# Two blocks on one core: recurrent levels one tile later, rotations between projected tiles, tails among attention blocks, bias rows as eight-row pieces

## The reference, cut to what matters

```
# first block, per direction
dt = softplus(dt_raw + dt_bias);  a_cum = cumsum(dt * A)          # per head and chunk
lmat = exp(segsum(a)) ; y_diag = (C B^T * lmat) @ (x * dt)
# second block, per layer (x2)
z = rmsnorm(h) @ w_in                                             # 18 tiles of 128 features
o_a = rmsnorm(hgrn2(hq, hf, hi, lb)) * sigmoid(hg)                # recurrent, 4 heads of 64
o_b = attention(rope(aq), rope(ak), av, sinks)                    # window 128, 8 heads, 2 kv heads
o_c = gelu(su) * (W_s @ layernorm(gelu(sv)) + b_s)                # spatial gating
h = h + rmsnorm(concat(o_a, o_b, o_c) @ w_out)
```

## Time and profile before

| | |
|---|---|
| median of 3 runs | 2760.44 us (2758.29 to 2760.99) |
| profiled execution | 2757.06 us |
| its span, first to last instruction | 2755.2 us |
| mean granted TensorE clock | 0.980 |

### The profile page before, as it was taken

How to read it: one execution, slowest core, us unless ns; L and a number is a source line. 1 busy time by engine, 2 the same in 40 slices (tenths; PEclk the granted TensorE clock), 3 DMA queues, 4 the chain that set the end, 5 groups by cost and what they waited for, 6 DMA issues and landing times. The chain is left out here.

```text
span 2755.2 us, 33704 instructions
## 1 busy us (share of the span) xinstructions
PE 2620.8 (95%) x12468; PEld 2107.7 (76%) x12468; DVE 1109.0 (40%) x1679; ACT 1001.9 (36%) x1484; POOL 1288.0 (47%) x1664
## 2 busy tenths in 40 slices
PE   6999999899999999989999999999999989999997
PEld 3788767677888877767888877888877757888885
DVE  5588654544222037535222036322017554222015
ACT  5223323334323233454333235332233454333234
POOL 1233456555554543345455445555544335545543
PEclk8999999999999999999999999999999999999999
DMA  6222111132332322112323332333332102332322
GB/s 265 69 62 78 61 42 31 39 108 84 96 100 95 99 77 78 58 31 84 100 92 96 95 92 79 105 98 100 93 92 75 62 17 84 100 99 92 99 92 76
DMA packets 63335, 234.05 MB, mean 85 GB/s; under 512 B 7264, under 2 KB 7520, under 8 KB 62688
## 3 DMA queue, kind: packets, MB, share of 16 engines
q1 hardware_dynamic: 61056, 222.33, 25.7%
q10 hardware_dynamic: 2144, 9.80, 1.0%
HBM read 230.00 MB, written 2.10 MB: 84 GB/s over the span
## 5 line engine op out<-in xcount | busy, mean ns | idle before, releaser
L427 POOL TENSOR_TENSOR wlo<-raw,whi 128x256 fp32r<-128x256 f32 x1584 | 1175.4, 775 | 1304.9 <-ACT whi L530 1304.8
L1826 PE MATMUL banks<-xhi,whi 128*128 128x512 f32 x1920 | 752.0, 392 | 0.0
L1827 PE MATMUL banks<-xhi,wlo 128*128 128x512 f32 x1920 | 747.8, 389 | 0.0
L1836 PE MATMUL banks<-xlo,whi 128*128 128x512 f32 x1952 | 736.4, 393 | 9.4 <-DVE xlo L1118 9.3
L530 ACT ACTIVATE whi<-raw 128x1024 fp32r<-128x1024 f32 x396 | 415.4, 1054 | 358.0 <-PE banks L1836 346.7
L1836 PEld LDWEIGHTS banks<-xlo,whi 128*128 128x128 f32 x1952 | 366.3, 189 | 95.4 <-DVE xlo L1118 17.1
L1826 PEld LDWEIGHTS banks<-xhi,whi 128*128 128x128 f32 x1920 | 360.8, 188 | 79.2 <-issue 2.1
L1827 PEld LDWEIGHTS banks<-xhi,wlo 128*128 128x128 f32 x1920 | 360.8, 188 | 75.3 <-issue 1.0
L1826 PE MATMUL banks<-act_hi,whi 128*128 128x512 f32 x704 | 273.9, 389 | 0.0
L1827 PE MATMUL banks<-act_hi,wlo 128*128 128x512 f32 x704 | 273.9, 389 | 0.0
L1836 PE MATMUL banks<-act_lo,whi 128*128 128x512 f32 x704 | 273.9, 389 | 0.0
(11 more groups left out here) (418 smaller groups left out, 3222.8 us busy)
## 6 DMA issues: line engine op xcount, KB each, us to landing
raw<-in_stream SPq DMA_DIRECT2D x396, 512.0 KB, 3.5
ada_raw<-in_stream SPq DMA_DIRECT2D x24, 512.0 KB, 7.5
h<-in_x ACTq DMA_DIRECT2D x2, 2048.0 KB, 12.3
out<-h SPq DMA_DIRECT2D x4, 512.0 KB, 2.6
ctx_raw<-in_ctx ACTq DMA_DIRECT2D x1, 1024.0 KB, 19.9
dft_t<-in_dft_t ACTq DMA_DIRECT2D x1, 1024.0 KB, 5.0
ple_raw<-in_ple ACTq DMA_DIRECT2D x2, 512.0 KB, 3.5
mixpar<-in_mixpar ACTq DMA_DIRECT2D x2, 384.0 KB, 4.4
```

The source lines that it names most:

```text
L427: piece = pool.tensor_tensor(wlo[:, i, s], raw[:, i, s], whi[:, i, s].bitcast(F32), ALU.subtract)
L1826: pe.matmul(acc[acc_of[t]][:], whi[:, u % SLOTS, i], x_h, start=(k == 0), stop=False, skip_group_check=split)
L1827: pe.matmul(acc[acc_of[t]][:], wlo[:, u % SLOTS, i], x_h, start=False, stop=False, skip_group_check=split)
L1836: mm = pe.matmul(acc[acc_of[t]][:], whi[:, u % SLOTS, i], x_l, start=False, stop=(k == k_tiles - 1), skip_group_check=leading and m < leads)
```

## The change

Second block: scores of level 1 and later stand one projected tile later in TensorE's queue, and so do transposes, chunk states and outputs of the recurrence; the squares' sums of its norm move behind score 0 of the attention. DVE masks level n - 1 ahead of the factors of level n, and centres the gate before the last level's factors. ACT takes gelu and the output gate's sigmoid together ahead of the last level's exponentials. Rotations 0, 1 and 2 stand behind tiles 14, 15 and 16; 3 and 4 among the first scores. Norm, output and cast of the recurrence (`hgrn_norm`, `hgrn_out`, `hgrn_high`) and the cast of the gating (`gating_high`) move to blocks 0, 5, 7 and 2 of the attention's loops. Scores of even and odd blocks exchange their banks.

First block: `bias_rows` holds per head four rows of high and four of low parts, one for each chunk. ACT issues six DMAs that spread `dt[3]` over partitions (`bias_pieces`), copies them later, and DVE subtracts. TensorE multiplies once with 512 columns against `pairs`, whose four columns are each repeated 128 times. The positions are loaded later.

```diff
+    table[:, C_LOW] = -(np.arange(P) % 2)
...
-        bias_rows = at("bias_rows", CONST + 13 * KB, [SEQ], F32R)
+        bias_rows = at("bias_rows", CONST + 13 * KB, [DT_ROWS // 16, P], F32R)
+        bias_pieces = at("bias_pieces", DYN + 86 * KB, [DT_ROWS // 16, P])
...
-        rot_bank = [bank[i] for i in (2, 3, 4, 5, 7)]
+        rot_bank = [bank[i] for i in (2, 7, 4, 7, 6)]
...
@@ -651,22 +656,25 @@
                     act.activation(diff[:, g], bank[6 + g], ACT.Square).then_inc(*done("hg_act", ("hg_o_sq", (layer, g))))
 
             def hgrn_norm(layer):
-                inverse_root(*(((layer, "hg", g), 64, bank[4 + g], k_dec[:, g]) for g in range(2)))
-                act.activation(z[:, 6:8], z[:, 6:8], ACT.Sigmoid).then_inc(*done("hg_act", ("hg_out_gate", layer)))
-                log_and_exp()
+                inverse_root(*(((layer, "hg", g), 64, bank[4 + g], hg_inverse[:, g]) for g in range(2)))
 
             def hgrn_high(layer):
                 for g in range(2):
...
@@ -694,6 +702,13 @@
                         exps(i)
                     if 1 <= i <= 16:
                         turned(i - 1)
+                    if i == 0:
+                        hgrn_norm(layer)
+                        value_tokens()
+                    elif i == 2:
+                        gating_high(layer)
+                    elif i == 7:
+                        hgrn_high(layer)
                     if i >= 5 and (i - 5) % 4 == 0:
...
@@ -701,6 +716,7 @@
             def gating_gelu(layer):
                 act.wait_ge(*after("z", (layer, 11)))
                 act.activation(z[:, 8:12], z[:, 8:12], ACT.Gelu_apprx_tanh).then_inc(*done("sg_act", ("gelu", layer)))
+                act.activation(z[:, 6:8], z[:, 6:8], ACT.Sigmoid).then_inc(*done("hg_act", ("hg_out_gate", layer)))
                 log_and_exp()
...
@@ -818,16 +834,21 @@
                 wave_sines(2)
                 wave_sines(3)
                 act.wait_ge(*after("dt_step", ("dt_bias", 0)))
-                act.activation(bias_rows[:], dt[3][:, 0:SEQ], ACT.Copy).then_inc(*done("dt_act", "bias"))
+                for b in range(DT_ROWS // 16):
+                    for e in range(2):
+                        act.dma_start(bias_pieces[e::2, b], dt[3][16 * b:16 * b + 16, 0:SEQ].rearrange("r (i f) -> r i f", f=P))\
+                            .then_inc(ld["masks"], 16)
                 wave_high(2)
                 wave_high(3)
                 token_steps()
...
+                    if n == 1:
+                        act.wait_ge(ld["masks"], 16 * (1 + 2 * (DT_ROWS // 16)))
+                        act.activation(bias_rows[:, :, :], bias_pieces[:, :, :], ACT.Copy).then_inc(*done("dt_act", "bias"))
                     act.wait_ge(*after("state", n))
                     act.activation(h0[d][:, g * GC:(g + 1) * GC], bank[4 + n % 4][:, 0:GC], ACT.Copy).then_inc(*done("h0", n))
-                act.dma_start(pos[:].bitcast(I32), a["positions"].broadcast_to([P, SEQ])).then_inc(ld["pos"], 16)
...
@@ -851,6 +872,9 @@
                         if m in (6, 9):
                             act.wait_ge(*after("ssd_y", m - 4))
                         act.activation(zs[:, m], acc[acc_of[t]][:], ACT.Copy).then_inc(*done("zs", m, bank_of=t))
+                    if v == 0:
+                        act.wait_ge(*after("dt_step", ("dt_rows", 0)))
+                        act.dma_start(pos[:].bitcast(I32), a["positions"].broadcast_to([P, SEQ])).then_inc(ld["pos"], 16)
...
@@ -1037,25 +1061,27 @@
                         hgrn_gates(layer)
                         projected(4)
                         hgrn_logs(layer)
-                        for n in range(1, len(LEVELS) + 1):
+                        projected(5)
+                        hgrn_decays(layer, 1)
+                        for n in range(2, len(LEVELS)):
+                            projected(4 + n)
                             hgrn_decays(layer, n)
-                            projected(4 + n)
-                        hgrn_chunk_decays(layer)
+                        projected(11)
                         gating_gelu(layer)
+                        hgrn_decays(layer, len(LEVELS))
                         projected(12)
                         gating_squares(layer)
                         projected(13)
-                        hgrn_tokens(layer)
+                        hgrn_chunk_decays(layer)
                         inverse_root(((layer, "ln"), 2 * P, acc[3][:], tmp[2][:]))
                         projected(14)
+                        hgrn_tokens(layer)
                         projected(15)
-                        hgrn_out(layer)
                         gating_tokens(layer)
                         projected(16)
-                        hgrn_norm(layer)
+                        hgrn_out(layer)
+                        attention_masks(layer)
                         projected(17)
-                        gating_high(layer)
-                        hgrn_high(layer)
                         attention(layer)
...
@@ -1181,10 +1207,10 @@
             def hgrn_level(layer, n):
 
                 b = LEVELS[n - 1]
-                if n == 1:
-                    v.wait_ge(*after("hg_step", ("hg_cleared", layer)))
+                hgrn_masked(layer, n - 1)
+                if n == len(LEVELS):
+                    gating_center(layer)
                 v.wait_ge(*after("hg_exp", (layer, n)))
...
-                hgrn_masked(layer, n - 1)
...
@@ -1275,18 +1300,19 @@
                     v.wait_ge(*after("att_probs", ("att_den", (layer, i))))
                     v.reciprocal(st[:, 6], st[:, 5]).then_inc(*done("att_probs", (layer, i)))
 
-                rotate(0)
-                rotate(1)
                 for i in range(16 + 3):
                     if i < 16:
                         shifts(i)
-                    if i < 3:
-                        rotate(2 + i)
                     if 1 <= i <= 16:
                         probabilities(i - 1)
-                    if 3 <= i < 7:
-
-                        mix_low(layer, i - 3, hg_o[:, i - 3] if i < 5 else z[:, 8 + i - 5])
+                    if i < 2:
+                        rotate(layer, 3 + i)
+                    elif i in (3, 4):
+                        mix_low(layer, i - 1, z[:, 8 + i - 3])
+                    elif i == 5:
+                        hgrn_out(layer)
+                    elif i in (7, 8):
+                        mix_low(layer, i - 7, hg_o[:, i - 7])
                     if i >= 6 and (i - 6) % 4 == 0:
...
@@ -1455,9 +1481,6 @@
                 wave_low(1)
                 wave_form(2)
                 wave_form(3)
-                v.wait_ge(*after("dt_act", "bias"))
-                v.tensor_tensor(bias_rows[64:P], dt[3][64:P, 0:SEQ], bias_rows[64:P].bitcast(F32), ALU.subtract)\
-                    .then_inc(*done("dt_step", ("dt_rows", 0)))
...
+                v.wait_ge(*after("dt_act", "bias"))
+                v.scalar_tensor_tensor(bias_rows[:, :, :], bias_rows[:, :, :].bitcast(F32), table[:, C_LOW:C_LOW + 1],
+                                       bias_pieces[:, :, :], ALU.mult, ALU.add).then_inc(*done("dt_step", ("dt_rows", 0)))
...
+                v.tensor_tensor(pairs[:], ident[:, 0:P:2], ident[:, 1:P:2], ALU.add)
...
@@ -1744,17 +1771,19 @@
                         projected(5)
                         for n in range(1, len(LEVELS) + 1):
                             hgrn_level(layer, n)
-                            projected(5 + n)
+                            if n == 1:
+                                projected(6)
+                            projected(6 + n)
                         hgrn_chunk(layer)
-                        gating_center(layer)
-                        projected(13)
+                        projected(14)
                         gating_scale(layer)
-                        projected(14)
+                        rotate(layer, 0)
+                        projected(15)
                         hgrn_states(layer)
-                        projected(15)
+                        rotate(layer, 1)
                         projected(16)
                         gating_out(layer)
-                        hgrn_out(layer)
+                        rotate(layer, 2)
...
-                levels = len(LEVELS) + 1
-                if 5 <= m < 5 + levels:
-                    hgrn_scores(layer, m - 5)
+                levels = len(LEVELS) + 2
+                if m == 5 or 6 < m < 5 + levels:
+                    hgrn_scores(layer, 0 if m == 5 else m - 6)
...
                         turn(bank[6 + g], z[:, 4 + g]).then_inc(*done("hg_vt", (layer, g)))
+                    rotated(layer, 0)
                 elif m == 6 + levels:
 
...
+                    rotated(layer, 1)
...
+                        if g:
+                            pe.wait_ge(*after("att_roped", ("att_rot_terms", (layer, 1))))
...
+                    pe.wait_ge(*after("att_roped", ("att_rot_terms", (layer, 2))))
...
+            def rotated(layer, i):
+
```

(44 more changed lines are left out.)

53 lines of the change are left out of this document (25 added, 28 removed).

## The result

The changed kernel took 2742.97 us (median of 4 runs, 2741.53 to 2743.57), the kernel before 2759.36 us beside it; the ratio is 0.994, with 95% between 0.9923 and 0.9958. The forecast was 2729.7 us, 30.7 less than before; 16.4 came. The profiled execution took 2742.5 us around a span of 2740.7 us, 14.5 less than that of before, at a mean granted clock of 0.978 (before 0.980).

The account below looks back on a forecast made before the run. TensorE, busy 95% of the span, was taken as the bound. Terms -15.5 - 1.0 - 9.8 - 6.0 + 1.4 + 0.2 = -30.7 us, off the median 2760.44, gave 2729.7 us; range 2722 to 2742.

Parts of the forecast that it names:

- What bounds the kernel: Whole kernel: TensorE is busy 95% of the span, so a gain must shorten its queue or close a pause.
- Levels, -15.5 us: Second block, both layers: level scores one tile later remove TensorE's pause for DVE's masked copy, saving 15.5 us.
- what is late next?: Levels: check for a new wait; DVE needs 6.1 of 7.65 us from one level's scores to the next factors.
- The gelu wait: Column sums' wait for the gelu: the gelu moves several TensorE steps away from its reader, saving 1.0 us.
- Attention, -9.8 us: Attention of both layers: stage falls to 48.2 us, -5.7 inside and +0.8 outside, -4.9 per layer.
- the walk: Attention: four engine queues stepped through with trace durations, TensorE at 2.4 GHz: 48.9 us new, 54.7 old.
- rival A: Attention: clock falls behind one new pause; gain shrinks from 9.8 to about 2.3 us, 2737 us; chance 0.18.
- Bias rows, -6.0 us: First block's head loop: one 512-column matmul replaces four short ones, 0.30 us per head for 20 heads.
- their preparation, +1.6: First block: six transfers issued by ACT cost 1.4 us, a small DVE operation for `pairs` 0.2.
- B: Bias rows: repeated column streams at the short products' pace, no gain, preparation cost stays; 2736 us; chance 0.12.
- C: Attention, blocks 1 to 15, both layers: low clock holds throughout, slower than before at 2769 us; chance 0.04.
- D: Levels: delayed last-level exponentials or late tile 7 weights bring back about half of 15.5 us; 2737 us; chance 0.06.

Follow-up runs that it names:

- levels_undone: Changed kernel with scores of level 1 and later, and ACT's and DVE's steps with them, back in their old places: 2756.79 us, ratio to before 0.9999.
- tile5_first: Changed kernel with DVE's scaling of tile 5 ahead of the recurrence's cumulative sums instead of behind them: 2738.63 us, ratio to before 0.9934.
- before_filled: Kernel before, with unread products added in TensorE's attention pauses at blocks 0, 1, 5, 6, 9, 13 and 14: 2752.13 us, ratio to before 0.9979.
- fill_half: Changed kernel with two unread products ahead of the attention transposes of each of blocks 1, 5 and 7, none elsewhere: 2735.37 us, ratio to before 0.9916.

## Where the prediction was right and where it failed

**What bounds the kernel.** Right: TensorE's queue and its pauses. That the price of a pause is read from repeating starts, because of the clock behind it, was right too, and was then not carried through for the attention.

**Levels, -15.5 us.** The mechanism was right: there is no wait for the masked copy, scores 1 at 1062.76 and the next at 1070.41, 7.65 us apart as forecast. levels_undone prices it at 13.0. The missing 2.3 us are a new wait that the question "what is late next?" passed over. I followed DVE's new order for the factors of the next level, and not for the bank that `projected(5)` frees. tile5_first gives the 2.3 us back. The gelu wait went as forecast.

**Attention, -9.8 us.** This is the step that failed, by 13.5 us in the two layers' stages together: 48.2 us each were forecast, 55.6 and 54.1 measured. The events of the walk were right: transposes of block 0 at +8.4 us (forecast 8.1), of block 1 at +11.6 (11.7), pauses of 1.73, 2.22 and 1.72 us at blocks 1, 5 and 7 (2.25, 2.2, 2.5), and 49.9 us for the stage with the clock at 1.00 (48.9). What was wrong is the pair of numbers that was subtracted. The new order was walked at 2.4 GHz, the old one, 54.7 us, with its measured low stretch in it. The same walk for the old order at 2.4 GHz throughout gives 49.8, and before_filled measures 50.9. So nearly all of the 5.7 us per layer was the assumption that the clock would stay up, and the rearrangement itself was worth 0.9 by the walk and 1.0 by the runs. In its place the clock was granted at 0.82 and 0.84 of full speed where it had been 0.87.
The reason I gave for the clock, that the new pauses were nearer to one of 2.08 us in the first block behind which the matmuls stayed at full speed, compared lengths of single pauses. The one of 1.73 us at block 1 stood 12 us behind the last projected tile, with 0.54 and 0.68 us of standing still in between and short products; the one in the head loop stands among long products. Whether that is the reason no run shows; fill_half shows that length alone does not decide.
The Trainium skill, "TensorE: Matmul & The Clock Gate", section "A second HAM failure mode: psum-queue depth-cycling", tells of a kernel in which TensorE stands still briefly between groups so often that the clock swings between its two levels. The trace of the changed kernel agrees, with 0.53, 0.96, 0.50, 0.99, 0.50, 0.99 and 0.62 in seven stretches one behind the other. Weighed with the pauses that the walk had found, it spoke for rival A and against the forecast.

**Bias rows, -6.0 us, and their preparation, +1.6.** The mechanism was right: -5.75 and +2.24 in the trace of the changed kernel, 6.1 us less for the part alone by its ratio. That -5.75 lies so near -6.0 was luck. A head saves 0.41 us instead of 0.30, 8.2 us in all, and in the changed kernel a lower clock in the head loop took 2.5 of them back. An issue costs 0.60 to 0.64 us instead of 0.33 to 0.46. The upper end was one row picked from ACT's first issues in the kernel before, which took 0.40 to 0.57.

**The rivals.** A was the right one, its price was not. It had one low stretch of about 12 us and 52.3 to 53.2 us for the stage; there were four, and its 2737 us became 2743. Its sum had a slip too: 2.3 us is the middle of the stages' 1.4 to 3.2, and the 1.6 us that the change costs outside them, which the 9.8 has in it, are not taken off; with them A is 2738.8. The new wait of 2.3 us adds to that. B is excluded by the products of 0.21 and 0.22 us. C, the clock low throughout, didn't come: it rose again each time, at about 1168, 1181 and 1188. D did not come either; no wait for a last level's exponentials stands in the list of waits. The range ended at 2742 because A was priced with a single fall of the clock, and the new wait of tile 7 was in no rival.

## What to carry to other kernels

When two orders of work are compared by a walk, walk both at the same clock and put the clock's part in a term of its own with its own chance; here that term was nearly the whole gain. The same code can be granted different clocks, so compare several stages, or stages at the same granted clock, before a difference of 1 or 2 us is believed. Where TensorE has short products and pauses, cut its time at the same events before and after and look at the granted clock of each stretch, since the list of waits can look better while the stage gets longer. A few unread products in the pauses are a cheap test of whether the clock or the chain holds a stage (here 49.9 us instead of 55.6 and 54.1), and may be left in where they lie in time that is lost anyway; work moved into such a stage goes one piece to a block.

## What the runs showed of the hardware

- Added work shortened a stage. With 36 more TensorE instructions the granted clock went from 0.82 to 1.00, and 55.5 us became 49.9. Pauses of 1.1 to 2.2 us among short products were followed by a fall to 1.2 GHz, but not always: behind one of 1.89 us the clock fell in one layer and stayed in the other, with the same code.
- One order of work took 49.9 us at a granted clock of 1.00, 53.4 to 53.6 at 0.87 and 55.5 to 55.6 at 0.82.
- A moving operand that repeats each of four columns 128 times took 0.21 to 0.22 us for 512 columns, like any other.
- Six transfers from partitions to partitions, issued by ACT, held its queue 0.60 to 0.64 us each, about twice the 0.33 us of the positions' issue; ACT's first issues in the kernel before took 0.40 to 0.57.
- DVE's product of two SBUF operands took 1.40 us where it started behind GpSimd's scaling and 0.69 where it started ahead of it; then the scaling took 1.00 us instead of 0.61. A reduction of scores by DVE, which reads PSUM, took 0.68 in the midst of a scaling in the changed kernel. The Trainium skill, "SBUF — State Buffer", section "🔬 SBUF: two separate sides", has DVE and GpSimd share one pair of ports, held by one of them for a whole instruction, and counts a DVE operation with two SBUF inputs among those that need it. These rows agree: whichever started second took longer, and DVE's operation ended 0.55 us behind GpSimd's.
